# A hybrid decoder layer on one core: value products of four heads and the diagonal moved before a projection, the other four heads' values and the levels grouped in pairs

## What is computed

```
proj = h @ w_in                      # queries, keys, values of 8 softmax heads (group A),
                                     # q, k, v, gate rg and decay of 4 gated linear heads (group B)
A: p = softmax(q k^T / 8 + alibi, causal);  o = p @ v                   # 8 heads of 64
B: b = cumsum(log_sigmoid(..)/16) per chunk of 64
   attn[t,s] = sum_d q[t,d] k[s,d] exp(b[t,d]-b[s,d])  for s <= t;      # 4 heads, key 64, value 128
   o = attn @ v (+ the state handed from chunk to chunk);  o = rmsnorm(o) * silu(rg)
x = LN1(alpha*x + concat(A, B) @ w_mix_o)
x = LN2(alpha*x + cross_attention(x, mem))   # 4 heads, 256 memory tokens, k, v = mem @ w_xkv
x = LN3(alpha*x + W2 relu(W1 x)^2)           # hidden 4096
```

## Time and profile before

| | before |
|---|---|
| median of 3 runs | 408.29 us |
| the profiled execution | 408.55 us |
| its span in the profile | 406.8 us |
| PE busy | 398.8 us (98%) |
| DVE busy | 280.5 us (69%) |
| ACT busy | 206.4 us (51%) |
| POOL busy | 63.0 us (15%) |
| mean granted TensorE clock | 0.997 of full |

### The profile page before, as it was taken

The page is one execution under the profiler, slowest core; times in us unless marked ns, Lnnn a source line. Parts: engine busy times, 40 slices in busy tenths (PEclk is TensorE's granted clock), DMA queues, the critical chain, the costliest instruction groups (busy, mean ns, idle before and its releaser), DMA issues.

```text
span 406.8 us, 5765 instructions
## 1 busy us (share of the span) xinstructions
PE 398.8 (98%) x2208; PEld 343.1 (84%) x2208; DVE 280.5 (69%) x363; ACT 206.4 (51%) x285; POOL 63.0 (15%) x61
## 2 busy tenths in 40 slices
PE   8999999999999999999999999999999999999993
PEld 4888888899988888899988888888888888888882
DVE  3699476998794796968658859383746475664826
ACT  5676578646354628555733457362725343444400
POOL 2039300046960105000005100000000000000000
PEclk9999999999999999999999999999999999999998
DMA  8998637635535380746265184655665637464002
GB/s 289 299 390 312 235 122 266 238 118 208 183 128 206 106 308 2 264 151 207 106 200 170 59 296 131 215 177 204 207 208 176 237 110 260 146 222 191 0 0 103
DMA packets 32364, 75.70 MB, mean 186 GB/s; under 512 B 1526, under 2 KB 3926, under 8 KB 32342
## 3 DMA queue, kind: packets, MB, share of 16 engines
q1 hardware_dynamic: 31952, 75.24, 53.3%
q10 hardware_dynamic: 390, 0.17, 0.3%
HBM read 74.35 MB, written 1.05 MB: 185 GB/s over the span
## 4 chain that ended last, share of the span: by engine, by line
PE 97%; DMA 1%; DVE 1%; issue 0%; DVEq 0%; ACT 0%; SPq 0%
PE bank L1339 20%; PE bank L1341 19%; PE bank L1340 19%; PE bank L1712 13%; PE bank L1413 8%; PE bank L1717 7%; PE bank L1417 4%; PE bank L1540 2%; PE bank L1345 1%; DMA raw<-in_w_in 1%; PE bank L1492 1%; PE bank L1518 0%; PE bank L1573 0%; PE bank L1625 0%; PE bank L1484 0%; PE bank L1483 0%
## 5 line engine op out<-in xcount | busy, mean ns | idle before, releaser
L890 DVE TENSOR_TENSOR w_lo<-raw,w_hi 128x2048 fp32r<-128x2048 f32 x36 | 83.8, 2333 | 15.2 <-ACT w_hi L544 15.2
L1274 DVE TENSOR_TENSOR w_lo<-raw,w_hi 128x2048 fp32r<-128x2048 f32 x24 | 55.0, 2291 | 40.3 <-ACT w_hi L827 40.3
L544 ACT CAST w_hi<-raw 128x2048 fp32r<-128x2048 f32 x38 | 72.2, 1915 | 18.7 <-PE bank L1341 14.3
L1339 PE MATMUL bank<-w_hi,actB_hi 128*128 128x512 f32 x192 | 75.7, 394 | 0.0
L1340 PE MATMUL bank<-w_lo,actB_hi 128*128 128x512 f32 x192 | 74.9, 390 | 0.0
L1341 PE MATMUL bank<-w_hi,actB_lo 128*128 128x512 f32 x192 | 74.8, 390 | 0.0
L827 ACT CAST w_hi<-raw 128x2048 fp32r<-128x2048 f32 x24 | 46.0, 1917 | 38.2 <-PE bank L1341 38.2
L1712 PE MATMUL bank<-actA,w_hi 128*128 128x512 f32 x224 | 53.3, 390 | 0.0
L1712 PEld LDWEIGHTS bank<-actA,w_hi 128*128 128x128 f32 x224 | 41.6, 188 | 8.3
L1341 PEld LDWEIGHTS bank<-w_hi,actB_lo 128*128 128x128 f32 x192 | 36.1, 188 | 7.6
L1339 PEld LDWEIGHTS bank<-w_hi,actB_hi 128*128 128x128 f32 x192 | 36.1, 188 | 7.1
(11 more groups left out here) (192 smaller groups left out, 617.6 us busy)
## 6 DMA issues: line engine op xcount, KB each, us to landing
raw<-in_w_ff SPq DMA_DIRECT2D x32, 1024.0 KB, 5.5
raw<-in_w_in SPq DMA_DIRECT2D x10, 1024.0 KB, 8.4
raw<-in_w_xkv SPq DMA_DIRECT2D x8, 1024.0 KB, 5.0
raw<-in_w_mix_o SPq DMA_DIRECT2D x4, 1024.0 KB, 4.7
raw<-in_w_xq SPq DMA_DIRECT2D x4, 1024.0 KB, 5.0
raw<-in_w_xo SPq DMA_DIRECT2D x4, 1024.0 KB, 4.8
raw<-in_w_in SPq DMA_DIRECT2D x4, 512.0 KB, 6.2
probs<-in_ln_g SPq DMA_DIRECT2D x3, 512.0 KB, 6.2
```

Source lines behind the costliest of these rows:

```text
L544: act.copy(dst, half_view(u)).then_inc(hi_done, 1)
L890: dve.tensor_tensor(dst, half_view(u), hi_part.bitcast(f32), ALU.subtract).then_inc(lo_done, 1)
L1274: dve.tensor_tensor(w_lo[:, c % 2, half, :], raw[:, u % RAW, :], w_hi[:, c % 2, half, :].bitcast(f32), ALU.subtract).then_inc(lo_done, 1)
L1339: pe.matmul(dst, stat[0], mov[0], start=start, stop=False, skip_group_check=on)
```

## The change

It leaves every product as it is and moves them, in five places:

- PE issues `pv0` and `diag` right behind the transposes of heads 4 to 7, ahead of `rg1`; `pv0` now lies in bank 0 and `diag` in bank 1.
- PE issues `pv1` between the two halves of `xk1`, followed by levels 0 and 1; it lies in bank 7.
- Levels 2 and 3 stand behind `xk2`, levels 4 and 5 inside `xv00`, level 6 and `off` inside `xv01`.
- ACT copies `diag` ahead of the cast of the weight half (6, 1), takes `pv1` behind the cast of half (7, 1), and casts half (9, 0) ahead of the last `decay`.
- DVE takes `pv1` behind the subtraction of half (7, 0) and merges the levels in pairs.

```diff
-    + [("rg1", 3), ("pv0", 4), ("pv1", 5), ("diag", 6), ("xk0", 0), ("xk1", 1)]
+    + [("pv0", 0), ("diag", 1), ("rg1", 3), ("xk0", 0), ("xk1", 1), ("pv1", 7)]
     + [("lv0", 4), ("lv1", 5), ("xk2", 2), ("lv2", 6), ("lv3", 7), ("xk3", 3), ("lv4", 4), ("lv5", 5),
-       ("xv00", 0), ("lv6", 6), ("off0", 7), ("off1", 4), ("xv01", 1), ("av0", 5), ("av1", 6)]
+       ("xv00", 0), ("xv01", 1), ("lv6", 6), ("off0", 7), ("off1", 4), ("av0", 5), ("av1", 6)]
@@ ACT
             for h in range(4, 8):
                 transposed(h)
+            b = wait_full(act, "diag")
+            act.copy(diag[:], b[:, 0:8]).then_inc(freed("diag"), 1)
             hi_half(6, 1)
             exp_r(1)
...
             mix(0, "pv0")
-            mix(1, "pv1")
-            b = wait_full(act, "diag")
-            act.copy(diag[:], b[:, 0:8]).then_inc(freed("diag"), 1)
...
             memk(0)
             hi_half(7, 1)
+            mix(1, "pv1")
             decay(2)
...
             memk(3)
+            hi_half(9, 0)
             decay(7)
...
-            hi_half(9, 0)
             evacuate("xv00", memv[:, 0, 0:512])
@@ DVE
             lo_half(6, 1)
             silu(1)
             mix(0, "pv0")
-            mix(1, "pv1")
             exponents(2)
             lo_half(7, 0)
+            mix(1, "pv1")
             exponents(3)
             lo_half(7, 1)
             masked(0)
+            masked(1)
             exponents(4)
-            masked(1)
             lo_half(8, 0)
             exponents(5)
+            lo_half(8, 1)
             masked(2)
-            lo_half(8, 1)
+            masked(3)
             exponents(6)
-            masked(3)
             exponents(7)
             masked(4)
             masked(5)
+            lo_half(9, 0)
             masked(6)
-            lo_half(9, 0)
             lo_half(9, 1)
@@ PE
+            def values_of(n):
+                b = begin(f"pv{n}")
+                for h in range(4 * n, 4 * n + 4):
+                    wait_out(pe, f"pt{h}")
...
+            def diagonal():
+                b = begin("diag")
...
             for h in range(4, 8):
                 transpose_probs(h)
+            for name in ("va0", "va1"):
+                wait_out(pe, name)
+            values_of(0)
+            diagonal()
             tokens(5, 1, A, "rg1")
...
             features(6, 0, B, "xk0")
-            features(6, 1, B, "xk1", between=lambda: level(0))
-            level(1)
-            features(7, 0, B, "xk2", between=lambda: level(2))
-            level(3)
-            features(7, 1, B, "xk3", between=lambda: level(4))
-            level(5)
-            tokens(8, 0, B, "xv00", between={4: lambda: level(6)})
-            off()
-            tokens(8, 1, B, "xv01")
+            def values_and_levels():
+                values_of(1)
+                levels(0, 1)
+
+            features(6, 1, B, "xk1", between=values_and_levels)
+            features(7, 0, B, "xk2")
+            levels(2, 3)
+            features(7, 1, B, "xk3")
+            tokens(8, 0, B, "xv00", between={4: lambda: levels(4, 5)})
+            tokens(8, 1, B, "xv01", between={4: last_level})
```

More of the change, by code:

```diff
@@ L1493, in transpose_probs @@
                 i.then_inc(full(f"pt{h}"), 1)
+            def values_of(n):
+                b = begin(f"pv{n}")
+                for h in range(4 * n, 4 * n + 4):
+                    wait_out(pe, f"pt{h}")
+                for h in range(4 * n, 4 * n + 4):
+                    r = slice(64 * (h % 2), 64 * (h % 2) + 64)
+                    c = (h // 2 - 2 * n) * S
+                    pe.matmul(b[r, c:c + S], va[:, 0, h * DA:(h + 1) * DA], probsT[:, h * 384:h * 384 + S],
+                              start=True, stop=False)
+                    i = pe.matmul(b[r, c + P:c + S], va[:, 1, h * DA:(h + 1) * DA],
+                                  probsT[:, h * 384 + S:h * 384 + 384], start=False, stop=True)
+                i.then_inc(full(f"pv{n}"), 1)
+            def diagonal():
+                b = begin("diag")
+                pe.wait_ge(qkdiag_done, 1)
+                pe.wait_ge(headsel_done, 2)
+                for t in range(2):
+                    for f in range(2):
+                        k = 4 * t + 2 * f
+                        i = pe.matmul(b[:, k:k + 2], qkdiag[:, f * S + t * P:f * S + (t + 1) * P], headsel[:],
+                                      start=True, stop=True)
+                i.then_inc(full("diag"), 1)
             tokens(3, 0, A, "va0")
@@ L1555, in _, with levels, last_level @@
             features(6, 0, B, "xk0")
-            features(6, 1, B, "xk1", between=lambda: level(0))
-            level(1)
-            features(7, 0, B, "xk2", between=lambda: level(2))
-            level(3)
-            features(7, 1, B, "xk3", between=lambda: level(4))
-            level(5)
-            tokens(8, 0, B, "xv00", between={4: lambda: level(6)})
-            off()
-            tokens(8, 1, B, "xv01")
+            def levels(*which):
+                for n in which:
+                    level(n)
+            def last_level():
+                level(6)
+                off()
+            def values_and_levels():
[7 more added lines that the diff above has]
+            tokens(8, 1, B, "xv01", between={4: last_level})
             for name in ("vg0", "vg1", "off0", "off1", "lv6"):
```

## The result

The changed kernel takes 417.1 us (median of 5 runs, 416.76 to 418.0) beside 408.32 for the kernel before. The ratio is 1.0208, 95% interval 1.0197 to 1.0219: 8.8 us slower. Its profiled execution took 417.56 us.

The account below looks back on a forecast made before the run. The prediction took PE to bound the kernel, busy 398.8 of 406.8 us. Its terms 4.85 + 1.55 + 0 + 1.65 + 0 = 8.05 us on 408.55 profiled gave 416.6, hence 416.3 us as median, range 414.5 to 419.0.

Parts of the forecast that it names:

- The likeliest case: The forecast itself: PE waits for bank 0 and the clock falls in that wait; 416.3 us, chance 0.62.
- The wait for bank 0: On PE ahead of `xk0`: DVE reads `pv0` only behind `silu(1)`, so `xk0` starts at about 90.0, not 85.19; +4.85 us.
- The cast of half (6, 1): On ACT, now behind the copy of `diag`: ends at about 80.6, wanted by DVE at 82.62, hidden by 2 us.
- The clock: PE's clock falls to half speed in the 6.1 us wait and needs 3.3 us to recover; +1.65 us.
- The values of heads 4 to 7: `pv1` now comes behind the start of `xk0`: 1.30 us of work plus 0.24 for its own entry and exit; +1.55 us.
- The pairs: Levels paired on PE, so fewer changes between plain float32 and fp32r products: 0 us, at most 0.3 saved.
- The levels' chain: Later work on DVE, ACT and POOL stays hidden from PE with 0.8 to 1.6 us to spare: 0 us.
- the lo half (7, 1): On DVE behind `pv1`: done by 106.4, wanted by PE at about 108 in `xk2`.
- The fourth level: On POOL: done by 112.4, wanted by PE at about 113.2.
- the second rival: A second wait follows on the levels' chain, or the low clock lasts twice as long: 417.5 to 420.5 us, chance 0.19.
- the first (no low clock): The clock doesn't fall within PE's wait, or only for a moment: 414.7 us, chance 0.15.
- the third (bank free in time): Bank 0 is free before `rg1` ends, so only merged groups and the second narrow group count: 408.1 us, chance 0.04.

Follow-up runs that it names:

- Experiment 1: The changed kernel with the banks of `pv0` and `diag` exchanged (`pv0` in bank 1, `diag` in bank 0): 409.55 us, ratio 1.0021.
- experiment 5: The changed kernel with useless plain float32 products on PE between `rg1` and `xk0`: 415.41 us with six; an earlier try with twelve overran the wait, 419.51 us.
- experiment 6: The kernel before with only `pv0` and `diag` moved ahead of `rg1` (banks 0 and 1), `pv1` behind `rg1`, levels single: 415.41 us, ratio 1.0168.
- experiment 4: The changed kernel with DVE reading `pv0` ahead of `silu(1)` instead of behind it: 411.83 us, ratio 1.0079.
- experiment 2: The kernel before with the levels two by two and `pv0`, `pv1` and `diag` not moved: 408.8 us, ratio 1.0000.
- experiment 3: The kernel before with each level's four products issued singly between the large products, 21 more changes of product kind: 409.53 us, ratio 1.0015.

## Why the prediction was right

The forecast was 416.3 us, range 414.5 to 419.0; measured were 417.1. The likeliest case came, and each step can be set beside its measure:

- **The wait for bank 0.** Forecast +4.85, measured 4.86 (first to second mark). The chain was read right link by link: `rg1` out at 84.2 (84.1), DVE's reading done at 90.04 (89.94 and the 0.1 of this execution). The cast of half (6, 1) began at 78.73 (78.6) and stayed hidden. Experiment 1 shows the cause: with another bank the wait is gone.
- **The clock.** Forecast that it would fall, and a loss of 1.65; it fell, and the loss is 2.27 (experiment 5, 56.01 - 53.74). The term was mis-sized in two ways that partly cancel. I took the time to full speed from the start of the program, 3.3 us, where it took 5.1 here (experiment 6 had 3.2 in the same place). And I booked half of it as lost, with products 0.24 apart; they stood 0.213 apart instead of 0.12, so a us at the low clock loses 0.44 and not 0.5: 5.15 * 0.44 = 2.27, and 3.2 * 0.44 = 1.4 in experiment 6, as measured. That the forecast of this term was near is in part luck, since one reading is no value for these times. At the end of the run the clock fell 3.0 us after the last product in one trace (experiment 4) and 5.0 in another (experiment 1), with the other eight in between. The same columns as in the stretches above, experiment 4 first (its last product is out at 403.6), then experiment 1 (402.0):

```profile
403.00:404.00 1.00, 0.61 (x3) 1.00 0.58 219
404.00:406.50 2.50, 0.00 (x0) 1.00 0.00 0
406.50:407.00 0.50, 0.00 (x0) 0.58 0.00 0
```

```profile
401.00:402.00 1.00, 0.98 (x5) 1.00 0.96 356
402.00:407.00 5.00, 0.00 (x0) 1.00 0.21 77
407.00:407.50 0.50, 0.00 (x0) 0.53 0.73 279
```

At the start, read from the spacing of the first products as in the earlier trace rows, full speed came from 3.0 us (experiment 6) to some 6.1 us (experiment 1) after the first product. The page "TensorE: Matmul & The Clock Gate" of the Trainium skill (Part 1) says that the moment of the change varies with a window that runs free of the kernel, by 0.5 us either way at the rise. The traces agree that it varies; by how much they do not: 3.0 to 5.0 us to the fall, 3.0 to 6.1 to the rise. Whether a free-running window is the reason no run shows.

- **The values of heads 4 to 7.** Forecast +1.55, measured 1.71 (53.74 - 52.03, experiment 5's span without the clock, which holds all of the new order). I booked 0.24 for the entry and exit and had left out the slower first records of a narrow group (0.48 in place of 0.43). The level behind the narrow group also takes 0.99 instead of 0.89; I had not seen that one coming.
- **The pairs.** Forecast 0, measured 0.02 (experiment 2) and nothing for 21 changes of kind (experiment 3).
- **The levels' chain.** Forecast hidden with 0.8 to 1.6 us to spare; no level waits in the changed kernel. The room was misread, though. The tightest link is not a level but the lo half (7, 1), forecast done 1.6 us ahead of PE. DVE began `pv1` 0.8 later than forecast (103.50), its exponents and this half took longer (2.83 where 2.28 is usual), and PE's first product that wants the half follows its end by 0.24 us:

```profile
105.85 2.83 DVE L890 TENSOR_TENSOR w_lo<-raw,w_hi 128x2048 fp32r<-128x2048 f32 x1
108.92 0.28 PE L1339 MATMUL bank<-actB_hi,w_hi 128*128 128x256 f32 x1
```

The fourth level, forecast to have 0.8 us, had 3.0 (POOL done at 111.1, PE there at 114.13). So the second rival came nearer than its account says, and by another link. Its 3.6 us for a product of POOL was a row of two products; single ones took up to 2.5 in the kernel before.

The sum was 8.05 and is 4.86 + 2.27 + 1.71 = 8.84; the 0.8 us between are the clock's 0.62, the narrow group's 0.16 and nothing else of size.

Of the rivals, the first (no low clock) is what experiment 5 made by force, 415.4 us; the second (a second wait) did not come; the third (bank free in time) is what experiment 1 made, 409.55 us. That is 0.8 us above the kernel before where the rival had 0.2 below it: 0.4 of saving that doesn't exist, 0.25 too little for the narrow group, and the wait for bank 1. It is still 0.21% slower than before, so the change holds no gain even with its fault mended: what it saves is nothing, and it adds a narrow group and a wait of 0.27 us. None of the versions run beats the kernel before. `pv1` put back beside `pv0`, ahead of `rg1`, was not tried.

## What to carry to other kernels

When a result is moved in a hand-made bank table, look up for each bank who reads the result ahead and where that reading stands in its engine's queue: the reader's place, not the producer's, sets when the next result may start. A wait of PE can be dearer than it is long, since the clock may fall and the products behind it then take 1.8 times their time for 3 to 5 us: waits of 5.9 and 4.4 us cost 2.3 and 1.4 us more here, one of 2.0 us nothing in its trace. No length is shown to be safe: the time to the fall was anything from 3.0 to 5.0 us in the traces, and one untraced execution with the wait of 2.0 us seems to have paid too. And before booking a saving for fewer changes between kinds of products, add the steps on both sides: a late successor can be the other end of an early start.

## What was not expected of the hardware

- The time from the last product to the fall of the clock was 4.2 us in both long waits and 3.0 to 5.0 at the end of ten runs; the time from PE's start to full clock was 5.1 and 3.2 behind the waits and 3.0 to some 6.1 at the start of the program.
- At the low clock these products of 256 columns stood 0.213 us apart, 1.8 times the 0.12 at the full clock and not twice.
- Products of 64 columns in the array's two halves, issued in turn, took 0.11 us per record of 256 columns; one half alone took about twice that, which made a head apart from the others cost 0.99 us instead of 0.33.
- The first group of plain products behind a narrow group took 0.99 us for 8 records where it takes 0.89 elsewhere.
